# The low half of a chunk, made one round later on VectorE: gating, convolution, retention and LRU

## What is computed

```
# first block ("mixer", then a product-key expert layer with 128 x 128 experts)
proj = rmsnorm(x) @ w_in
attn  = windowed attention, 6 heads;  mem = cross attention, 4 heads
xc    = 4-tap depthwise convolution of x_l
lru   = (h_fwd + h_bwd) * gelu(gate_l)        # bidirectional RG-LRU, 6 blocks of 128
y     = gates * [attn @ p_attn, lru @ p_lru, mem @ p_mem], summed, @ w_out
x     = x + y, then the experts, then rmsnorm

# second block, two layers
z  = rmsnorm(x) @ w_in
ya = silu(ga) * groupnorm(retention(q, k, v)) * gn_g       # 4 heads
yb = silu(layer_norm(depthwise_conv31(a * sigmoid(g))))    # 4 chunks of 128 channels
yc = u * (w_s @ layer_norm(v) + b_s)                       # spatial gating, 4 chunks
yd = sliding-window attention, 8 heads
x  = x + (sum_n sigmoid(zg_n) * (y_n @ w_branch_n)) @ w_out
x  = x + (silu(h @ w_gt) * (h @ w_up)) @ w_ffn_out
```

## Time and profile before

| | us |
|---|---|
| median of 3 runs | 2213.82 |
| lowest and highest | 2213.49, 2218.5 |
| the profiled execution | 2220.73 |
| its span in the trace | 2219.0 |
| PE busy in it | 2164.4 (98%) |
| DVE busy | 1342.0 (60%) |
| ACT busy | 1229.2 (55%) |
| POOL busy | 972.2 (44%) |
| mean granted clock of PE | 0.992 |

### The profile page before, as it was taken

One profiled execution on the slowest core, in us unless ns is written; L12 is line 12 of the kernel. 1 busy time (PEld: TensorE's weight loads), 2 busy tenths in 40 slices (PEclk: granted clock), 3 DMA queues, 4 the chain that ended last, 5 costly groups with the idle time before them and its releaser, 6 DMA issues.

```text
span 2219.0 us, 38752 instructions
## 1 busy us (share of the span) xinstructions
PE 2164.4 (98%) x15172; PEld 2029.8 (91%) x15172; DVE 1342.0 (60%) x2580; ACT 1229.2 (55%) x2201; POOL 972.2 (44%) x791
## 2 busy tenths in 40 slices
PE   8998999999999999999999998999999999899999
PEld 7898889999999988888889898999998999799997
DVE  3547652998666756666666754356654864446664
ACT  5667554456777755455454555644445455555443
POOL 4675546999666640000007775450002776461000
PEclk9999999999999999999999999999999999999999
DMA  6543455666444556666656553365565545355665
GB/s 208 157 143 117 154 185 170 188 182 180 142 143 143 145 188 191 194 193 193 196 172 198 157 170 117 122 190 151 182 190 171 173 147 161 105 162 169 183 184 158
DMA packets 102952, 370.16 MB, mean 167 GB/s; under 512 B 11370, under 2 KB 12786, under 8 KB 102132
## 3 DMA queue, kind: packets, MB, share of 16 engines
q1 hardware_dynamic: 102772, 367.69, 54.4%
HBM read 365.53 MB, written 2.11 MB: 166 GB/s over the span
## 4 chain that ended last, share of the span: by engine, by line
PE 86%; DVE 6%; ACT 4%; issue 1%; POOL 1%; DMA 1%; SPq 0%; DVEq 0%; ACTq 0%; POOLq 0%
PE stream_bank L556 16%; PE stream_bank L558 15%; PE stream_bank L557 15%; PE side_bank L556 10%; PE side_bank L557 10%; PE side_bank L558 10%; PE side_bank L809 1%; PE side_bank L808 1%; ACT unit_hi L1068 1%; PE side_bank L618 1%; DVE swa_var L2228 1%; POOL unit_lo L2352 1%; PE side_bank L637 1%; PE side_bank L657 1%; DVE unit_lo L1611 1%
## 5 line engine op out<-in xcount | busy, mean ns | idle before, releaser
L2352 POOL TENSOR_TENSOR unit_lo<-raw,unit_hi 128x512 fp32r<-128x512 f32 (+1 forms) x724 | 932.9, 1314 | 426.8 <-ACT unit_hi L1068 425.2
L1068 ACT ACTIVATE unit_hi<-raw 128x1024 fp32r<-128x1024 f32 (+1 forms) x678 | 708.5, 1045 | 196.3 <-PE side_bank L558 84.6
L1611 DVE TENSOR_TENSOR unit_lo<-raw,unit_hi 128x1024 fp32r<-128x1024 f32 (+1 forms) x316 | 389.2, 1232 | 271.5 <-ACT unit_hi L1068 271.1
L556 PE MATMUL stream_bank<-hT_hi,unit_hi 128*128 128x256 f32 x1672 | 491.5, 294 | 4.3 <-POOL unit_lo L2352 4.3
L557 PE MATMUL stream_bank<-hT_lo,unit_hi 128*128 128x256 f32 x1672 | 476.2, 285 | 0.0
L558 PE MATMUL stream_bank<-hT_hi,unit_lo 128*128 128x256 f32 x1672 | 476.1, 285 | 0.0
L556 PEld LDWEIGHTS stream_bank<-hT_hi,unit_hi 128*128 128x128 f32 x1672 | 323.1, 193 | 12.4 <-POOL unit_lo L2352 5.5
L556 PE MATMUL stream_bank<-h2T_hi,unit_hi 128*128 128x256 f32 x1152 | 329.6, 286 | 0.0
L558 PE MATMUL stream_bank<-h2T_hi,unit_lo 128*128 128x256 f32 x1152 | 326.0, 283 | 0.0
L557 PE MATMUL stream_bank<-h2T_lo,unit_hi 128*128 128x256 f32 x1152 | 325.8, 283 | 0.0
L557 PEld LDWEIGHTS stream_bank<-hT_lo,unit_hi 128*128 128x128 f32 x1672 | 323.3, 193 | 1.6
(11 more groups left out here) (342 smaller groups left out, 4096.3 us busy)
## 6 DMA issues: line engine op xcount, KB each, us to landing
raw<-in_peer_u_dram SPq DMA_DIRECT2D x128, 512.0 KB, 3.6
raw<-in_peer_v_dram SPq DMA_DIRECT2D x128, 512.0 KB, 4.2
raw<-in_gate_dram SPq DMA_DIRECT2D x64, 512.0 KB, 3.6
raw<-in_gt_dram SPq DMA_DIRECT2D x44, 512.0 KB, 3.6
raw<-in_up_dram SPq DMA_DIRECT2D x44, 512.0 KB, 3.6
raw<-in_ffn_out_dram SPq DMA_DIRECT2D x44, 512.0 KB, 3.8
raw<-in_branch_dram SPq DMA_DIRECT2D x32, 512.0 KB, 3.6
raw<-in_w_gate_dram SPq DMA_DIRECT2D x24, 512.0 KB, 3.6
```

The lines of the kernel that those rows point to most:

```text
L556: mm(out, l.hi, r.hi, start=start, stop=False)
L1068: activation(k.unit_hi[n % SPLIT_SLOTS][:, 0:w], k.raw[n % RAW_SLOTS][:, 0:w], ACT.Copy).then_inc(k.sem("unit_hi"), 1)
L1611: V.tensor_tensor(k.unit_lo[s][:, 0:w], k.raw[n % RAW_SLOTS][:, 0:w], k.unit_hi[s][:, 0:w], ALU.subtract).then_inc(unit_lo, 1)
L2352: last = G.tensor_tensor(k.unit_lo[s][:, cols], k.raw[n % RAW_SLOTS][:, cols], k.unit_hi[s][:, cols], ALU.subtract)
```

## The change

In each of the four generators of DVE's program the `yield` moves from behind the low half to ahead of it. The number of instructions, of signals and of yields stays as it was, and no other engine's program changes. The wait for ACT's high half and the subtraction now come at the start of the generator's next step, after the next unit's step of `main`, and ahead of whatever that generator does next.

```
 lru_scan:
             V.tensor_tensor(t1[:, 0, :], t1[:, 0, :], k.gl[:, i, :], ALU.mult).then_inc(k.sem("lru_gated"), 1)
+            yield
             dve.wait_ge(k.sem("lru_hi"), i + 1)
             V.tensor_tensor(k.branch.lo[:, 6 + i, :], t1[:, 0, :], k.branch.hi[:, 6 + i, :], ALU.subtract).then_inc(
                 k.sem("lru_lo"), 1)
-            yield
 convolution:
                 V.tensor_tensor(u, u, var, ALU.mult).then_inc(k.sem("conv_normed"), 1)
+                yield
                 dve.wait_ge(k.sem("conv_hi"), n)
                 V.tensor_tensor(k.ys.lo[:, 4 + i, :], u, k.ys.hi[:, 4 + i, :], ALU.subtract).then_inc(k.sem("conv_lo"), 1)
-                yield
 gating:
                 V.tensor_tensor(u, k.bank[SIDE + 4][:, 0:TOKENS], u, ALU.mult).then_inc(k.free[SIDE + 4], 1)
+                yield
                 dve.wait_ge(k.sem("gating_hi"), n)
                 V.tensor_tensor(k.ys.lo[:, 8 + i, :], u, k.ys.hi[:, 8 + i, :], ALU.subtract).then_inc(k.sem("gating_lo"), 1)
-                yield
 retention_head:
             V.scalar_tensor_tensor(ga, b[:, 0:TOKENS], k.col(name("gn"), h), ga, ALU.mult, ALU.mult).then_inc(
                 k.free[SIDE + 2], 1)
+            yield
             dve.wait_ge(k.sem("ret_hi"), g + 1)
             V.tensor_tensor(k.ys.lo[:, h, :], ga, k.ys.hi[:, h, :], ALU.subtract).then_inc(k.sem("ret_lo"), 1)
-            yield
```

## The result

Five timed executions of the changed kernel have a median of 2195.95 us (2192.43 to 2202.65), against 2215.81 for the kernel before in the same comparison: a ratio of 0.9905 (95% interval 0.9890 to 0.9920), 19.9 us less. Forecast were 17.2 us less and 2196.6. Run once more beside the last experiment, the same kernel gave 2193.82 against 2217.95, a ratio of 0.9892 (0.9875 to 0.9908). The profiled execution is the fastest of the first five (2192.43, span 2190.7), that of before was a long one (2220.73), so the two traces differ by 28.3 us, 8.4 more than the medians. I therefore compare stages rather than spans. Much of the 8.4 is PE's clock in other stages. Outside the layers' windows the trace of before has five short stretches at the low clock, at about 189, 229, 810, 1182 and 1506 us; that of after has none from 20 to 2190.

What follows compares the result with a forecast made beforehand. PE was taken as the bound, so only its idle time and lower-clock losses count. Idle time 10.2 + clock 6.7 - retention 1.2 + mixer 1.5 = 17.2 us off 2213.8, giving 2196.6; 8-in-10 range 2188 to 2208.

Steps and rivals of the forecast that it cites:

- What bounds the kernel, and where: PE is busy 2164.4 of 2219.0 us, so only its idle time, some 55 us, and lower-clock losses can be won.
- The convolution's rounds: Four per layer: 4.48 us leave DVE's chain, less 1.07 for three low halves meeting POOL; gating's first product 1.27 earlier.
- my own rival without the meeting: DVE's low half issues just before POOL's piece, so nearly all 7.05 a layer go: 2190 to 2192 us; chance 0.13.
- The three gaps: PE's idle of 0.94, 2.13 and 3.98 us in each layer's 38 us window; 5.1 of 7.05 to go, 10.2 in all.
- ACT would become the bound: At the 3.98 gap, ACT's exponentials, waiting for the head's maximum, bound next; transposes start 5.1 to 5.2 us earlier.
- The 0.94: PE gap before the attention scores, which wait for scaled queries coming 1.55 us earlier; the gap goes.
- the 2.13: PE gap before gating's second chunk, ended by DVE's first gating product; stays near 1.8 to 2 us.
- the 3.98: PE gap before the head's transposes, ended by ACT's normalisation; some 0.2 us of it stays.
- The clock: From first head's transposes to output in each layer, full clock expected to hold: 3.35 us a layer, 6.7 in all.
- The rival (the clock falls all the same): The remaining 2 us gap is enough to lower PE's clock; 10.5 us gained, 2203 us; chance 0.2.
- Retention: Four heads a layer: low half added ahead of the next head's normalisation, 0.6 us lost a layer, 1.2 in all.
- The mixer: LRU beside attention: in the first head's round 0.66 wait and 0.93 low half leave the chain, 1.5 us gained.

Runs made afterwards that it cites:

- e4: Only retention's and the LRU's low halves moved, convolution and gating as in the kernel before: 2214.68 us against 2217.39, ratio 0.9989.
- e1: Convolution and gating low halves moved, LRU and retention as in the kernel before: 2199.03 us against 2217.39, ratio 0.9920.
- e5: Changed kernel plus one tiny DVE instruction ahead of each convolution low half, so POOL's piece begins first: 2204.78 us against 2215.86 before, ratio 0.9946.
- e2: Only the convolution's low halves moved, the rest as in the kernel before: 2208.62 us against 2217.39, ratio 0.9963.
- e3: Only gating's low halves moved, the rest as in the kernel before: 2215.04 us against 2217.39, ratio 0.9987.
- e9: As e2, plus 11 useless PE matmuls ahead of the first head's wait for the normalisation: 2206.01 us against 2219.41 before, ratio 0.9944.
- e11: As e2, plus 6 useless PE matmuls ahead of the first head's wait for the normalisation: 2202.95 us against 2217.95 before, ratio 0.9931.
- e7: Changed kernel plus two unused DVE reciprocals behind the convolution's last low half, in each layer: 2205.76 us against 2215.86 before, ratio 0.9952.
- e10: Changed kernel with the mixer's attention step ahead of the LRU step on DVE and ACT: 2204.48 us against 2219.41 before, ratio 0.9929.

## Why the prediction was right

**What bounds the kernel, and where.** Right: e4 leaves layer 1 as it was, e1 takes it to the changed kernel's length. Of the waits of PE, what moved with the change lies at the attention's start in the layers and in the mixer. The clock's short falls in other stages, which only the trace of before has, are no part of the forecast.

**The convolution's rounds.** Here is the term that was mis-sized. I charged 1.07 to three of four low halves for meeting POOL and let gating's first product come 1.27 earlier. All four took 0.42 (L2117's four in layer 0 had a maximum of 0.419), and the product came 3.8 earlier: 18.30 us behind the first of the convolution instead of 22.10. Two low halves began 0.02 and 0.01 ahead of POOL's piece. The second shares its round with DVE's own unit (in the forecast I had put that one last). At the fourth a meeting was paid after all, but by the head's maximum ahead of it, which now falls beside POOL's pair: 1.06 once, not 1.07 three times. That leaves 4.48 - 1.06 = 3.42; the other 0.4 is overlap that comes back where a wait goes, since an instruction that follows another directly begins before that one has ended (L2117 at 1347.48, behind a scaling that runs to 1347.57), four times some 0.09. The maximum before and after:

```profile
1372.60 0.23 DVE L1668 TENSOR_SCALAR smalls<-smalls,cols 128x2 f32<-128x2 f32 x1
...
1360.63 1.29 DVE L1668 TENSOR_SCALAR smalls<-smalls,cols 128x2 f32<-128x2 f32 x1
```

So my own rival without the meeting is nearer to what happened than my forecast. The price was right (e5: 1.09 each), only the order could not be had from rows in which the low half stood elsewhere. I wrote that the low half comes "just as" POOL starts, and still put 0.13 on the one outcome; the two deserved even chances. Two slips in the working changed little: the tiny instruction of 1.21 in the earlier trace rows is an addition, not a subtraction, and that rival's sum counts retention at 0.8 where the forecast has 1.2.

**The three gaps.** Forecast 5.1 of 7.05 closed a layer, measured 6.35. The 0.94 went, the 2.13 went too instead of keeping some 2, and the 3.98 left 0.70, as ACT's wait, where I had 0.2: in layer 0 DVE's reciprocal ended at 1363.54, and ACT came to the normalisation at 1364.56, behind a weight copy, an eviction and gating's high half. That ACT would become the bound was right: with one delay of 1.74 on DVE the idle time rises by only 0.85.

**The clock.** Taken: 3.35 a layer. In the two traces compared it is 3.39 in layer 0. But it isn't certain, as I had it with the small gap left. Behind the same gap of 0.68 to 0.70, ten times in five traces, the output followed by 4.26 to 4.28 in five and by 5.75 to 5.79 in the other five, so the term is 1.7 to 3.4 a layer. In the layers of the kernels that had 1.28 or more of idle time there, not filled with matmuls, it fell every time. The rival (the clock falls all the same) was half right, at a smaller price.

**Retention.** Forecast 1.2 lost, measured nothing: L946's waits went from this, in the kernel before, to 2.9 in 2.

```profile
PE side_bank L946 <- DVE S L2180: 3.3, 4, 1.4
```

I had put the low half one round too late. It ran right behind the next head's statistics, ahead of ACT's root of them (L1467, at 1253.98), in a time in which DVE has nothing else to do (its next instruction comes at 1257.08):

```profile
1251.98 0.17 DVE L2194 TENSOR_SCALAR smalls<-smalls 128x2 f32<-128x2 f32 x1
1252.06 0.42 DVE L2216 TENSOR_TENSOR ys_lo<-ret_gate,ys_hi 128x256 fp32r<-128x256 f32 x1
```

**The mixer.** Forecast 1.5, and this was too little. In the trace the first head's gap fell from 4.37 to 1.96, more than I took. An earlier LRU chunk lost some of it again: its low half (at 145.62) met POOL, took 1.53 and held up the rotation of the queries, 1.5 at L726, which I hadn't seen. From the kernel's first keep-warm matmuls to the next ones (L607) the two traces compared take 315.0 and 312.5. The six traces with the LRU as before (before, e1, e2, e3, e9, e11) lie at 314.6 to 317.4 there, the six with all its low halves moved (the changed kernel twice, e4 to e7) at 310.5 to 313.1; the means differ by 3.5. e4's median, 2.7, agrees. A part of it is the clock, which I had only in the bounds: around the first head's transposes it fell in all six of the former, and in two (e5 and e7) of the latter.

**The sum.** By the traces: 2 x 6.35 for the idle time, 2 x (1.7 to 3.4) for the clock, 0 for retention, 2.5 to 3.5 for the mixer: 19 to 23. The measured 19.9 lies in it and 24.1 just beyond. The forecast's 17.2 had the idle time 2.5 too low, the mixer 1 to 2 too low, a loss of 1.2 that didn't come, and a clock priced as certain, up to 3.3 too high. The mechanism was the forecast one; that the number came so near is in part luck, as these errors have both signs.

## What to carry to other kernels

A wait of a helper engine for another helper is worth what PE's idle time behind it is worth, and in this kernel a gap was priced twice: once as idle time, and once more as the slow clock after it, so that two edits that each left a gap gained 11.2 singly and 18.4 together. Before moving the order of rounds, write out which step of which round stands ahead of the critical instruction; the order within a round (e10) doesn't change that by itself. Where two engines shut each other out and start within 0.1 us, give both orders equal chances, and keep the range between their sums.

## What the runs showed of the hardware that I had not expected

- A lead of 0.01 to 0.07 us decided who pays: 1.09 for a DVE subtraction of 128x256, 0.26 for POOL's pair of 128x512. Even DVE's maximum of 128x2 (L1668) took 1.29 beside POOL's pair and 0.23 without it.
- PE's clock fell behind a single gap of 0.70 in half of the cases. In the mixer it fell around the first head's transposes in all six traces with a gap of 4.4 there, and in two of the seven with a gap of 1.9 to 2.0. When it fell differs as well: behind the same gap of 4.37 the transposes began at the low clock in the kernel before, and at the full clock in e1, where it fell 0.9 us later. The transposes of both, and two windows of e1:

```profile
188.78 1.08 PE L648 MATMUL side_bank<-base_consts,S 128*128 128x128 f32 x4 [4.37 <-ACT S L1133]
187.44 0.63 PE L648 MATMUL side_bank<-base_consts,S 128*128 128x128 f32 x4 [4.37 <-ACT S L1133]
187.50:188.30 0.80, 0.80 (x6) 0.77 (x7) 0.55 (x3) 0.80 (x2) 0.00 (x0) 1.00 0.60 225
188.33:191.70 3.37, 3.37 (x15) 3.18 (x14) 3.27 (x5) 2.92 (x9) 0.37 (x1) 0.50 0.57 156
```

  The Trainium skill ("TensorE: Matmul & The Clock Gate", What's actually happening) says that the chip's watch on PE's activity runs freely and isn't tied to the kernel's start. That would make equal gaps fare differently, as here; no run shows the cause itself.
- Much of what looks like the spread of a kernel's runs goes with this: 1.5 us for each layer in which the clock falls, and more elsewhere. The changed kernel's first five runs took 2192.43 and 2193.89 us at a mean granted clock of 0.999, 2195.95 at 0.998, 2198.45 at 0.996 and 2202.65 at 0.995.
